# Modulation tiles one weight tile later, closed by transposes or by high and low parts; two subtractions moved in the second mixer

## The reference

```python
mod_x = jnp.split(jax.nn.silu(c) @ w_ada[l] + b_ada[l], 6, axis=-1)   # sh1, sc1, gt1, sh2, sc2, gt2
hx = modulate(rms_norm(x, norm1), sh1, sc1)
...
x = x + gt1[..., None, :] * branch_merge(attn_x, gla_x, ga, gg, w_br_attn, w_br_gla, w_out)
x = x + gt2[..., None, :] * sq_relu_mlp(modulate(rms_norm(x, norm2), sh2, sc2), w_mlp1, w_mlp2)

def branch_merge(attn, gla, gate_a, gate_g, w_br_attn, w_br_gla, w_out):
    y = jax.nn.sigmoid(gate_a) * (attn @ w_br_attn) + jax.nn.sigmoid(gate_g) * (gla @ w_br_gla)
    return y @ w_out
...
def mlstm_mixer(xn, w_in, b_gates, head_norm, w_out):     # q, k, v, o, gates from xn @ w_in; scan both ways
    ...
    return h.astype(xn.dtype) @ w_out
```

## Time and profile before

| what | value |
|---|---|
| runs | 915.5, 916.14, 916.28 us |
| the profiled execution | 916.24 us, span of its trace 914.3 us |
| PE busy | 889.6 us (97%) |
| PE weight loads busy | 761.7 us |
| DVE busy | 624.5 us (68%) |
| ACT busy | 479.6 us (52%) |
| DMA | 162.11 MB, mean 177 GB/s |
| chain that ended last | PE 83%, DVE 9%, DMA 3%, ACT 3% |

### The profile page before, as it was taken

The page is one execution under the profiler, slowest core; times in us unless marked ns, Lnnn a source line. Parts: engine busy times, 40 slices in busy tenths (PEclk is TensorE's granted clock), DMA queues, the critical chain, the costliest instruction groups (busy, mean ns, idle before and its releaser), DMA issues.

```text
span 914.3 us, 14123 instructions
## 1 busy us (share of the span) xinstructions
PE 889.6 (97%) x5120; PEld 761.7 (83%) x5120; DVE 624.5 (68%) x1002; ACT 479.6 (52%) x759; POOL 11.3 (1%) x22
## 2 busy tenths in 40 slices
PE   6899999999999999999999999999999999999995
PEld 2688888887788887889999998897888999999984
DVE  2568779779777878776555558667777855555576
ACT  3647545665656566464444444444655744444453
POOL 0200000000000000000000000000000000000000
PEclk9999999999999999999999999999999999999998
DMA  9864212335346777636555557353434765555531
GB/s 359 335 184 170 80 55 93 97 111 170 131 144 224 250 254 247 211 134 235 190 192 187 184 184 262 106 184 121 156 115 162 227 222 207 191 186 188 194 102 47
DMA packets 45377, 162.11 MB, mean 177 GB/s; under 512 B 5616, under 2 KB 5760, under 8 KB 45329
## 3 DMA queue, kind: packets, MB, share of 16 engines
q1 hardware_dynamic: 42896, 155.73, 50.2%
q0 software_dynamic: 1296, 4.02, 1.6%
q10 hardware_dynamic: 1136, 1.70, 0.5%
HBM read 160.39 MB, written 1.05 MB: 177 GB/s over the span
## 4 chain that ended last, share of the span: by engine, by line
PE 83%; DVE 9%; DMA 3%; ACT 3%; issue 1%; SPq 0%; DVEq 0%; ACTq 0%
PE bank L691 70%; DVE w_lo L1675 3%; DMA raw<-in_stream 1%; PE bank L946 1%; PE bank L863 1%; DMA arena<-in_early 1%; PE bank L853 1%; PE bank L1147 1%; ACT w_hi L1245 1%; PE bank L961 1%; PE bank L966 1%; DVE act_lo L1675 1%; PE bank L870 1%; PE bank L884 1%; PE bank L811 1%
## 5 line engine op out<-in xcount | busy, mean ns | idle before, releaser
L1675 DVE TENSOR_TENSOR w_lo<-raw,w_hi 128x1024 fp32r<-128x1024 f32 x244 | 288.2, 1220 | 161.7 <-ACT w_hi L1245 161.3
L1245 ACT ACTIVATE w_hi<-raw 128x1024 fp32r<-128x1024 f32 x244 | 245.1, 1050 | 197.7 <-PE bank L691 165.1
L691 PE MATMUL bank<-w_hi,act_lo 128*128 128x512 f32 x720 | 292.9, 407 | 0.3 <-DVE w_lo L1675 0.2
L691 PE MATMUL bank<-w_lo,act_hi 128*128 128x512 f32 x720 | 281.3, 391 | 0.0
L691 PE MATMUL bank<-w_hi,act_hi 128*128 128x512 f32 x720 | 280.8, 390 | 0.0
L691 PE MATMUL bank<-act_lo,w_hi 128*128 128x256 f32 x640 | 183.0, 286 | 3.4 <-DVE act_lo L1675 3.0
L691 PE MATMUL bank<-act_hi,w_hi 128*128 128x256 f32 x640 | 181.1, 283 | 0.0
L691 PE MATMUL bank<-act_hi,w_lo 128*128 128x256 f32 x640 | 181.0, 283 | 0.0
L691 PEld LDWEIGHTS bank<-w_lo,act_hi 128*128 128x128 f32 x720 | 135.1, 188 | 29.4
L691 PEld LDWEIGHTS bank<-w_hi,act_lo 128*128 128x128 f32 x720 | 135.5, 188 | 27.3 <-issue 1.7
L691 PEld LDWEIGHTS bank<-w_hi,act_hi 128*128 128x128 f32 x720 | 135.6, 188 | 26.0 <-issue 1.2
(11 more groups left out here) (253 smaller groups left out, 771.3 us busy)
## 6 DMA issues: line engine op xcount, KB each, us to landing
raw<-in_stream SPq DMA_DIRECT2D x278, 512.0 KB, 4.4
arena<-in_early SPq DMA_DIRECT2D x14, 512.0 KB, 12.4
res<-in_x ACTq DMA_DIRECT2D x1, 1024.0 KB, 9.1
raw<-in_early SPq DMA_DIRECT2D x2, 512.0 KB, 13.6
arena<-in_ctx SPq DMA_DIRECT2D x1, 1024.0 KB, 13.3
res<-in_x POOLq DMA_DIRECT2D x1, 1024.0 KB, 8.2
arena<-in_norm_final POOLq DMA_DIRECT2D x1, 512.0 KB, 3.9
arena<-in_ple_b POOLq DMA_DIRECT2D x1, 512.0 KB, 5.3
```

The lines of the kernel that those rows point to most:

```text
L691: last = pe.matmul(o, left, right, start=start and m == 0, stop=stop and m == 2, skip_group_check=shared)
L1245: return act.activation(o, i, ACT.Copy)
L1675: return dve.tensor_tensor(o, x, hi.bitcast(F32), ALU.subtract)
```

## The change

A modulation tile is summed one weight tile later: 7 moves from go0 to go1, 8 to ga1, 9 to wba0, 4 to wba1 and 5 to gg0; 10 stays in gg1. Tiles 6 to 9 are closed by four transposes into a PSUM bank, which DVE then reduces along the free axis. Tiles 4, 5 and 10 (`GT_PARTS`) are split like a weight: ACT writes the high part of the sum (at the place of its last unit), DVE the low part (a step "gtcut"), and PE multiplies each by a column of ones in fp32r that is read as a matrix; this closing stands after the next weight tile's second group. Tile 11 stays as it was. In the second mixer the fourth cut of mq moves behind the second half of "turn n3", and part b of head 1 moves ahead of the first cut of mv1.

```diff
+GT_PARTS = (4, 5, 10)
...
+            if i == 2:
+                self.steps += [("gtcut", int(m[3:])) for m in self.sums if int(m[3:]) in GT_PARTS]
             if i in sums:
                 self.steps.append(("ada", ada, sums.index(i)))
             if q == pieces(n, g) - 1:
                 self.steps.append(("evac", n, g))
-                if g == 0:
-                    for m in self.sums:
+                for m in self.sums:
+                    if g == int(int(m[3:]) in GT_PARTS):
                         self.steps += [("mm", m, 0, 0), ("evac", m, 0)]
+                if g == 1:
                     self.sums = []
...
-    p.woven("go0", [None, att[0], ("qkturn", 1), att[1], None] + att[2:6], ada=7)
-    p.woven("go1", att[6:14], ada=8)
+    p.woven("go0", [None, att[0], ("qkturn", 1), att[1], None] + att[2:6])
+    p.woven("go1", att[6:14], ada=7)
     out = out_steps()
-    p.woven("ga1", att[14:] + [("gosilu",), ("sigmoid", "ga0"), ("explog",), ("gomul",)], ada=9)
-    p.woven("wba0", out[:9], ada=4)
-    p.woven("wba1", [("sigmoid", "ga1"), ("explog",)] + out[9:18], ada=5)
-    p.woven("gg0", out[18:] + [("merge", "gla", h, 5) for h in range(2)])
+    p.woven("ga1", att[14:] + [("gosilu",), ("sigmoid", "ga0"), ("explog",), ("gomul",)], ada=8)
+    p.woven("wba0", out[:9], ada=9)
+    p.woven("wba1", [("sigmoid", "ga1"), ("explog",)] + out[9:18], ada=4)
+    p.woven("gg0", out[18:] + [("merge", "gla", h, 5) for h in range(2)], ada=5)
...
-              last(1, 1), ("cut", "mq", 2), ("cut", "mq", 3)])
+              last(1, 1), ("cut", "mq", 2)])
...
-    p.steps += [("mm", "mq", 0, 0), ("mm", "mq", 0, 1), ("turn", "n3", (2, 3)), ("round", "mk", 0), ("mm", "mq", 1, 0),
+    p.steps += [("mm", "mq", 0, 0), ("mm", "mq", 0, 1), ("turn", "n3", (2, 3)), ("cut", "mq", 3), ("round", "mk", 0), ("mm", "mq", 1, 0),
...
-    p.woven("mo0", [c[0], d[0], b[1], sq[0], a[2], c[1], d[1], sq[1]])
+    p.woven("mo0", [c[0], [d[0], b[1]], None, sq[0], a[2], c[1], d[1], sq[1]])
...
-                    if tile in GT_TILES:
-                        last = ada_fin(o, tile)
+                    if tile in GT_PARTS:
+                        every = ones_r[:, 0:1].broadcast_to([P, P])
+                        pe.wait_ge(gt_lo, GT_PARTS.index(tile) + 1)
+                        pe.matmul(o[:, :], every, small_hi[:, 0:NC], start=True, stop=False)
+                        last = pe.matmul(o[:, :], every, small_lo[:, 0:NC], start=False, stop=True)
                     else:
                         pe.wait_ge(ada_sum_done, ADA_ORDER.index(tile) + 1)
                         for b in range(4):
-                            last = pe.matmul(o[:, b:b + 1], ada_sum[:, b * P:(b + 1) * P], ones[:, 0:1],
-                                             start=True, stop=True)
+                            last = pe.transpose(o[:, b * P:(b + 1) * P], ada_sum[:, b * P:(b + 1) * P], ident)
...
+                elif kind == "ada" and step[1] in GT_PARTS and step[2] == 3:
+                    i = GT_PARTS.index(step[1])
+                    act.wait_ge(ada_sum_done, ADA_ORDER.index(step[1]) + 1)
+                    if i > 0:
+                        act.wait_ge(group_done, GROUP_AT[f"ada{GT_PARTS[i - 1]}", 0] + 1)
+                    hi_part(small_hi[:, 0:NC], ada_sum).then_inc(gt_hi, 1)
...
-                    c = 4 * int(n[3:])
-                    dve.tensor_tensor(mods[:, c:c + 4, 0], bank[:, 0:4], cols[:, C_ADA + c:C_ADA + c + 4],
+                    c, s = 4 * int(n[3:]), stat[:, 7, 0:4]
+                    chain(dve.tensor_reduce(s, bank[:, :].rearrange("p (b k) -> p b k", b=4), AX, ALU.add))
+                    dve.tensor_tensor(mods[:, c:c + 4, 0], s, cols[:, C_ADA + c:C_ADA + c + 4],
                                       ALU.add).then_inc(evac_dve, 1)
...
+                elif kind == "gtcut":
+                    i = GT_PARTS.index(step[1])
+                    dve.wait_ge(gt_hi, i + 1)
+                    lo_part(small_lo[:, 0:NC], ada_sum, small_hi[:, 0:NC]).then_inc(gt_lo, 1)
```

More of the change, by code:

```diff
@@ L145, in woven @@
             upto = (i + 1) * len(side) // len(parts)
-            self.steps += [s for s in side[done:upto] if s]
+            for s in side[done:upto]:
+                self.steps += s if isinstance(s, list) else [s] if s else []
             done = upto
@@ L404, in build @@
         strips = sb("strips", [P, 2])
+        ones_r = sb("ones_r", [P, 1], F32R)
         psum = [ctx.enter_context(nc.psum_tensor(f"bank{i}", [P, NC], F32)) for i in range(8)]
@@ L548, in build @@
         ada_sum_done = sem("ada_sum_done")
+        gt_hi, gt_lo = sem("gt_hi"), sem("gt_lo")
         gain_ready = sem("gain_ready")
@@ L1080, in m_gates @@
                     pe.wait_ge(mg_rows, 1)
-                    pe.wait_ge(pick_ready, 2)
+                    pe.wait_ge(pick_ready, 3)
                     for t in range(TT):
@@ L1588, in _ @@
                     hi_part(mg_w[:, :, 0:16], small[:, 256:384].rearrange("p (k n) -> p k n", k=KC)).then_inc(small_hi_done, 1)
+                    hi_part(ones_r[:, :], ones[:, 0:1]).then_inc(pick_ready, 1)
                     hi_part(pick_r[0:GH, :], ident[0:GH, 0:GH]).then_inc(pick_ready, 1)
@@ L1592, in _ @@
                     act.wait_ge(small_lo_done, 2)
+                    act.wait_ge(group_done, GROUP_AT["ada10", 0] + 1)
                     hi_part(small_hi[:, 0:512], p_in).then_inc(small_hi_done, 1)
+                elif kind == "ada" and step[1] in GT_PARTS and step[2] == 3:
[4 more added lines that the diff above has]
+                    hi_part(small_hi[:, 0:NC], ada_sum).then_inc(gt_hi, 1)
                 elif kind == "pcut":
```

## The result

The changed kernel took 931.03 us (median of 4 runs, 930.2 to 933.26) against 916.21 us (915.5 to 916.97, 4 runs) for the kernel before: a ratio of 1.0162, 95% interval 1.015 to 1.0174. It is 14.8 us slower. The forecast was 928.2 us, with a range of 924 to 932. The profiled execution took 930.74 us, with a span of 928.9 us; before, it took 916.24 us.

What follows compares the result with a forecast made beforehand. PE, busy 97% of the span, was taken to set the time. Chain and tile 10's closing +11.9, clock +1.4, second mixer -1.2 gave +12.1 us on 916.1: 928.2 us, range 924 to 932.

Steps and rivals of the forecast that it cites:

- the chain: In gg0, gg1 and wbg0, DVE, ACT and PE wait on each other in turn; PE 11.9 us late after tile 10's closing.
- (a): Rival: nothing in gg0 to wbg0 is late and only the savings count, 910.9 us; chance 7%.
- (b): Rival: PE loses only the first stall of 5.65 us, the yturn's input being ready in time, 918.1 us; chance 8%.
- PE's own savings: At the closings: 1.2 us from three fp32r closings at 0.46 each, 1.8 us from four closings by transposes.
- go0 and the second mixer: The late low part's wait in go0 goes, 1.0 us back; two waits in the second mixer go, 1.2 us together.
- DVE starts the sum of tile 5: In gg0, DVE begins summing tile 5 at 331.4 us, bounds 330.9 and 332.5.
- `small_lo` of tile 5 done: DVE finishes tile 5's low part, behind the second cut of wbg0, at 347.45 us.
- sum of tile 10 done: DVE ends tile 10's four units, one head step and the bias at 356.85 us.
- first yturn of PE: PE arrives at 356.4 us, waits for DVE's steps that finish wbg0's first half, and goes on at 366.6 us.
- first and second stall: PE waits 5.65 us before tile 5's closing at gg1's end, then 10.2 us before the first yturn.
- (c): Rival: blocked loads, or further waits in wba1, make tile 10's units late, 4 us on top, 932 us; chance 10%.
- The clock: PE's granted clock falls in the second stall and costs 1.4 us on the way up, bounds 0 and 3.

Runs made afterwards that it cites:

- e5: Changed kernel with ACT's high part of a sum moved to the place of DVE's low part, behind the rounds: 924.97 us, ratio 1.0102.
- e4: Kernel before with only the new closings of tiles 4, 5 and 10 by high and low parts, tiles at old places: 931.1 us, ratio 1.0161.
- e6: Changed kernel with ACT's high part behind the rounds and the next sum waiting for the low part, not PE's closing: 921.37 us, ratio 1.0057.
- e9: Changed kernel with five idle fp32 matmuls ahead of tile 5's closing and eleven ahead of the first yturn: 929.76 us, ratio 1.0144.
- e3: Kernel before with only the later places of the modulation tiles, closings as before: 920.69 us, ratio 1.0058.
- e1: Kernel before with only the two moved subtractions of the second mixer: 914.96 us, ratio 0.9989.
- e2: Kernel before with only tiles 6 to 9 closed by transposes and a reduction, at old places: 915.12 us, ratio 0.9991.
- e7: Changed kernel with old places, ACT's high part behind the rounds, buffer freed before the closing, tile 10's low part later: 914.49 us, ratio 0.9979.
- e8: Changed kernel with four idle fp32 matmuls ahead of tile 5's closing and eight ahead of the first yturn: 930.38 us, ratio 1.0161.

## Why the prediction was right

**The direction and the chain.** Right, and shown by three runs: with the high part behind the rounds the loss falls from 14.8 to 9.0 us, with the buffer freed as well to 5.4 (by the medians; the traces don't show that step), and with both and the old places and a later low part of tile 10 it is gone. The rival of the savings alone (a) and that of one stall (b) fall, since both stalls are in the trace. That ACT and DVE take their queues in order is what e5 shows: the same instruction behind the rounds instead of ahead of them is worth 6.1 us. It agrees with the Trainium skill, page "TensorE: Matmul & The Clock Gate", section "Architectural detail: the array is 16× 32×32, not 1× 128×128", which calls both strictly first in, first out.

**PE's own savings.** The fp32r closing of tile 4 in the changed kernel, by starts:

```profile
332.03 0.40 PE L753 MATMUL bank<-small_hi,ones_r 128*128 128x512 f32 x1
332.26 0.40 PE L754 MATMUL bank<-small_lo,ones_r 128*128 128x512 f32 x1
332.50 0.39 PE L698 MATMUL bank<-w_hi,act_lo 128*128 128x512 f32 x1
```

0.47 us, as taken (0.46). The weight load that reads one column as a matrix costs nothing more. The four transposes of tile 8 take 0.67 from their start at 289.52 to the second weight matmul at 290.19, less one of 0.23: 0.44, as taken. None of it reaches the end, since the yturn waits for DVE whenever PE comes.

**go0 and the second mixer.** The wait in go0 is gone: between 82 and 233 us PE gains 1.15 us, against 1.0 forecast. The second mixer gives 0.60 at each place, together the 1.2 of the sum.

**The chain, term by term.** (forecast, then measured)

| step | forecast | measured |
|---|---|---|
| DVE starts the sum of tile 5 | 331.4 | 332.70 |
| `small_lo` of tile 5 done | 347.45 | 348.2 |
| sum of tile 10 done | 356.85 | 358.4 |
| first yturn of PE | 366.6 | 367.79 |
| first and second stall | 5.65, 10.2 | 4.9, 8.3 |

The start was 1.3 us late, outside its bounds by 0.2, and this is the step that I missed. I held that PE and DVE reach the end of gg0 at about the same time and put no wait there. But the head's steps of DVE (line 2085) stand behind the sum of tile 4, two cuts and its low part, so PE waited 1.82 us at line 991, closed tile 4 later, and DVE waited 3.05 us for that closing. Rival (c) comes nearest: it named further waits of the kind, but put them in wba1, and late loads, of which one of 0.77 us is in the sum of tile 10; its 4 us on top did not come. The start's 1.3 us reached the yturn as 1.2. The stalls are shorter than forecast because PE itself came later to both: to the first by the 1.8 us, to the second also by the slow clock behind the first (0.73 in the window 343 to 350, with matmuls 0.43 us apart until 352.8), which the second stall hides, as the prediction had it.

**The clock.** The mis-sized term. I took 1.4 us from the kernel's first matmuls, within bounds of 0 and 3. Filling the idle time gave 2.66, inside the bounds. The first matmuls were the wrong measure: they are slow for 3.4 us, while behind the stall of 8.3 us PE worked for 5.7 us at 0.50, from 367.79 to about 373.5.

**Sum.** By the trace: +12.70 at the first yturn, +3.18 to the second (0.46 closing, 2.66 clock, 0.06 unexplained), -1.20 in the second mixer, -0.18 elsewhere: +14.5, which is 930.74 - 916.24. Forecast were 11.45, 1.86, -1.2 and 0: +12.1. Of the 2.4 us between them half is the missed wait and half the clock.

## What to carry to other kernels

When an instruction is put on an engine that works in order, ask first how long it will wait there and what stands behind it, and only then what it saves: here an ACT instruction of 0.6 us for each of three tiles, put ahead of the rounds, cost 6 us. A single buffer that is freed by the last reader of a three-engine chain makes one tile's delay the next one's start (DVE waited 3.05 us for it here), so find the earliest point at which it can be freed. And before counting a saving on the busiest engine, look whether its next wait has slack: here of a saving of 1.7 us, 0.6 was gone at the next join.

## What the runs showed of the hardware

The granted clock fell to 0.50 after short waits too, and not always at the same length: with the closings alone (e4) after waits of 3.7 and 2.3 us, in e5 after 2.2, in e6 after 3.8, in e9 after 2.06 us, but not after 1.82 us in the changed kernel, and not in e3 after 2.6 us. Such a fall cost 1.6 us where I worked it out (e9); behind the 8.3 us stall it cost 2.66.

The profiled executions of four kernels (e1, e2, e7 and e9) also show a fall at about 40 us, before anything that they change. PE waits 1.31 to 1.36 us there, until 38 us. The changed kernel, e3, e4, e5 and e6 have the same wait of 1.30 or 1.31 us, and the kernel before and e8 one of 1.54, without a fall. So here the length of the last wait does not tell whether the clock falls. In e9 the windows have 0.50 at 40 to 42 us, and the lateness goes from -0.4 to +1.1 us. It moves single executions by 1.2 to 1.5 us, which is as much as several of the effects measured here, so lateness was always compared within one trace.
